# Taking the barriers out of a three-stage decoder-layer kernel: weights as bf16 images in DRAM, SBUF slots reused tile by tile

## The reference

```python
h = rmsnorm(x, norm1_w);  z = h @ w_in                    # (S, 5632)
q, k, v, xr, yr, ga, gr = split(z)                        # 512,512,512,1024,1024,1024,1024
o_attn = moba_attention(rmsnorm(q), rmsnorm(k), v, rel_bias)   # 8 heads of 64, block 256, own block + top 3 past blocks
xr = causal_depthwise_conv(xr);  o_rnn = rg_lru(xr) * gelu(yr) # linear recurrence over the tokens
merged = sigmoid(ga + b0) * (o_attn @ w_proj_attn) + sigmoid(gr + b1) * (o_rnn @ w_proj_rnn)
x = x + merged @ w_out
x = x + square(relu(rmsnorm(x, norm2_w) @ w_ff1)) @ w_ff2      # 1024 -> 4096 -> 1024
```

## Time and profile before

| | us |
|---|---|
| median of 3 runs (2818.44 to 2821.68) | 2819.83 |
| the profiled execution, its own time | 2818.97 |
| its span on the slowest core (core 4) | 2817.3 |
| spans of the 8 cores | 2802.9 to 2817.3 |
| PE busy | 2478.8 (88%) |
| ACT busy | 1573.3 (56%) |
| DVE busy | 1112.8 (39%) |
| POOL busy | 287.8 (10%) |

### The profile page before, as it was taken

The page is one execution under the profiler, slowest core; times in us unless marked ns, Lnnn a source line. Parts: engine busy times, 40 slices in busy tenths (PEclk is TensorE's granted clock), DMA queues, the critical chain, the costliest instruction groups (busy, mean ns, idle before and its releaser), DMA issues.

```text
span 2817.3 us, 37218 instructions; the slowest of 8 cores (2802.9 to 2817.3 us)
## 1 busy us (share of the span) xinstructions
PE 2478.8 (88%) x12206; PEld 1116.8 (40%) x12434; DVE 1112.8 (39%) x1860; ACT 1573.3 (56%) x2339; POOL 287.8 (10%) x310
## 2 busy tenths in 40 slices
PE   1888899999988458999999999956999999999999
PEld 0444444444433113444443443422444444444444
DVE  1764444342200166677677677321122122221221
ACT  0567788989899377788779778132122132231220
POOL 1000000000000122222112112020001011010110
PEclk9999999999999779999999999977999999999999
DMA  6211101100000690211220220297211211112101
GB/s 106 90 57 49 42 16 53 38 16 31 5 8 1 138 135 1 83 40 46 80 83 16 68 83 9 89 181 134 75 46 45 83 38 60 60 45 75 46 30 53
DMA packets 66921, 165.82 MB, mean 59 GB/s; under 512 B 7283, under 2 KB 27932, under 8 KB 65692
## 3 DMA queue, kind: packets, MB, share of 16 engines
q1 hardware_dynamic: 38028, 129.60, 14.3%
q0 software_dynamic: 28704, 33.82, 8.3%
HBM read 151.07 MB, written 46.15 MB: 70 GB/s over the span
## 4 chain that ended last, share of the span: by engine, by line
PE 76%; ACT 9%; issue 5%; DMA 4%; DVE 4%; another core or an unknown queue 1%; POOL 0%; SPq 0%; ACTq 0%; DVEq 0%; POOLq 0%
PE bank L422 76%; ACT arena L422 9%; DVE arena L422 4%; DMA arena<-w_in 1%; ACT L422 1%; DMA arena<-x 1%; DMA arena<-out 1%; DMA arena<-scr_w 1%; POOL arena L422 0%; DMA arena<-c_G 0%; SPq L427 0%; DMA scr_w<-arena 0%; ACTq L247 0%; DMA scr_o<-arena 0%
## 5 line engine op out<-in xcount | busy, mean ns | idle before, releaser
L422 PE MATMUL bank<-arena 128*128 128x512 bf16 (+8 forms) x12206 | 2478.8, 357 | 334.5 <-DVE arena L422 112.8
L422 PEld LDWEIGHTS bank<-arena 128*128 128x128 bf16 (+4 forms) x12434 | 1116.8, 99 | 1695.9 <-issue 622.5
L422 ACT ACTIVATE arena<-bank 128x1024 bf16<-128x1024 f32 (+3 forms) x1024 | 786.0, 795 | 725.7 <-PE bank L422 717.5
L422 ACT ACTIVATE arena<-arena 128x512 f32<-128x512 f32 (+5 forms) x642 | 375.9, 599 | 105.4 <-DMA arena<-x 52.6
L422 DVE TENSOR_TENSOR arena<-bank,arena 64x512 bf16<-64x512 f32 (+3 forms) x218 | 137.0, 641 | 664.0 <-PE bank L422 598.1
L422 DVE SCALAR_TENSOR_TENSOR arena<-arena 128x512 f32<-128x512 f32 (+2 forms) x321 | 276.2, 866 | 232.1 <-ACT arena L422 227.1
L422 DVE TENSOR_TENSOR arena<-arena 128x512 bf16<-128x512 f32 (+2 forms) x324 | 212.3, 656 | 326.6 <-ACT arena L422 316.2
L422 POOL TENSOR_TENSOR arena<-arena 128x512 bf16<-128x512 f32 x176 | 212.2, 1206 | 1222.2 <-ACT arena L422 458.2
L422 DVE SCALAR_TENSOR_TENSOR arena<-arena,bank 128x512 f32<-128x512 f32 x256 | 173.1, 681 | 125.8 <-ACT arena L422 65.8
L422 ACT ACT_TABLE_LOAD x129 | 165.5, 1283 | 96.8 <-POOL arena L422 48.0
L422 ACT ACTIVATE arena<-bank,arena 128x512 f32<-128x512 f32 x256 | 166.4, 684 | 61.6 <-PE bank L422 39.9
(11 more groups left out here) (17 smaller groups left out, 69.8 us busy)
## 6 DMA issues: line engine op xcount, KB each, us to landing
arena<-x SPq DMA_DIRECT2D x64, 512.0 KB, 4.2
out<-arena SPq DMA_DIRECT2D x64, 512.0 KB, 2.9
arena<-out SPq DMA_DIRECT2D x64, 512.0 KB, 4.2
arena<-w_ff POOLq DMA_DIRECT2D x16, 1024.0 KB, 75.7
arena<-w_in POOLq DMA_DIRECT2D x11, 1024.0 KB, 30.8
scr_h<-arena SPq DMA_DIRECT2D x32, 256.0 KB, 3.2
arena<-scr_h SPq DMA_DIRECT2D x8, 1024.0 KB, 4.9
scr_o<-arena SPq DMA_DIRECT2D x8, 512.0 KB, 3.8
```

Of the source, the lines that this page charges most:

```text
L422: return P.add(eng, lambda e, m=meth, kw=kw: getattr(e, m)(**kw), reads, writes, cost=cost, fam=fam)
```

## The change

What it does, part by part:

1. **Images.** 27 DRAM tensors `img_*` are added. For every weight except `wqkv` and the small block-diagonal ones, one DMA on the POOL queue reads the float32 weight and writes it as bf16 to its image, DRAM to DRAM. They are issued during stage A: the one for tile t waits until the keys of tile t-1 are made. `load_w` later moves an image into SBUF as it is, from the SP queue.
2. **No barriers.** Every SBUF region has a fixed offset and a second or third tenant. `P.alias` names, for each new tile, the old tiles whose readers and writers its first write must wait for.
3. **Loads placed ahead.** Four of the recurrence's weight tiles, `wbda`, `wbdi` and the first `hTs` are loaded in chunk 6 of stage A; the rest of stage B's weights right behind the last attention result. `W1` is loaded in chunks 6 and 7 of stage B, `W2` behind stage B's last stores. The front end of stage C's chunk 0 (`FECt`) stands between the gatings of chunk 7.
4. **Start.** The loads of x tiles 0 and 1 stand first on SP. The four loads and matmuls of the bias table become one load of 1 MB and four matmuls behind the first FE. `c_E` (the 16 rows that carry the block mask into the keys) and `pvec` move behind the first FE.
5. **Cost model.** The scheduler's costs of ACT and POOL instructions change (89 ns for a scale or bias that is a tile), and its model of DMA: one pipe for each queue, at 140 B/ns for POOL and 340 B/ns for the others, in place of one common pipe at 270. So the order of instructions differs in all stages.

```diff
+            for k in writes:
+                for old in self.alias.pop(k, ()):
+                    j = last_w.get(old)
+                    if j is not None:
+                        d.add(j)
+                    d.update(readers.get(old, ()))
...
-                    xfer = nb / 270.0
-                    t0 = max(st + cost, dma_pipe)
-                    dma_pipe = t0 + xfer
+                    xfer = nb / (140.0 if e == 'gpsimd' else 340.0)
+                    t0 = max(st + cost, dma_pipe[e])
+                    dma_pipe[e] = t0 + xfer
...
+        def load_w(nm):
+            img, dst = image[nm]
+            dma('sync', dst.rearrange("p a b -> p (a b)"), img, 'ld_' + nm, ['im_' + nm], [nm])
...
+                for nm, img, src in imaged[t:t + 1] if t else ():
+                    dma('gpsimd', img, src, 'im_' + nm, ['kT%d' % (t - 1)], ['im_' + nm])
...
+            FE(0, 0)
+            for g in range(4):
+                op('tensor', 'matmul', ['hk', 'Js'], ['B%d' % (3 + g)], out=bankf[3 + g], lhsT=Js, rhs=hk[:, 2 * g:2 * g + 2, :],
+                   start=True, stop=True)
...
+            dma('sync', kT[64:80, :, :], cE_d.rearrange("n (h s) -> n h s", h=NH, s=S), 'c4', [], ['kTE'])
+            dma('sync', pvec, pvec_d.rearrange("p (t j) -> p t j", t=8, j=11), 'c0c', [], ['pvec'])
+            for tl in range(1, TPC):
                 FE(0, tl)
...
+                    if c == NCH - 2 and h == 5:
+                        dma('sync', nw, nw_d[:, D:2 * D], 'c0g', [], ['nw', 'nw2'])
+                        for nm in ('wr0', 'wr2', 'wr1', 'wr3'):
+                            load_w(nm)
...
         if 2 in phases:
-            P.barrier()
-            AR.reset(mP)
...
+                    if c == NCH - 1:
+                        if m == 0:
+                            for tl in range(3):
+                                load_xC(0, tl)
+                        if m % 2 == 1:
+                            FECt(0, m // 2)
...
+                        if m < 4:
+                            load_w('w1_%d' % (m + 4))
...
         if 3 in phases:
-            P.barrier()
-            AR.reset(mP)
...
+            for g in (0, 1, 2, 6, 7, 3, 4, 5):
+                load_w('w2_%d' % g)
```

More of the change, by code:

```diff
@@ L399, in op @@
                     if eng == 'scalar':
-                        cost = nel * 0.8333 + 105.0
-                        if 'out' in kw and kw['out'].dtype == F32 and nel >= 256:
-                            cost += 70.0
+                        cost = nel * 0.8333 + (98.0 if ref_ap.dtype == BF16 else 170.0)
+                        for o_ in ('scale', 'bias'):
+                            if o_ in kw and not isinstance(kw[o_], float):
+                                cost += 89.0
                     elif eng == 'vector':
@@ new lines, in build_nc @@
+        oaTs = [AR.alloc([4, CH], BF16), AR.at(RA + 36 * K, [4, CH], BF16)]
+        assert AR.off <= RK + 32 * K
+        ornTs = [AR.at(RK + 32 * K, [8, CH], BF16), AR.at(RA + 8 * K, [8, CH], BF16)]
+        wpa = AR.at(RV, [4, D], BF16)
+        wpr = AR.at(RV + 8 * K, [8, D], BF16)
+        wo = AR.at(RV + 24 * K, [8, D], BF16)
+        mT = AR.at(RV + 40 * K, [8, CH], BF16)
+        xres = [AR.at(RA + (24 + 4 * i) * K, [D], F32) for i in range(3)]
+        kTh = ['kTh%d' % h for h in range(4)]
@@ new lines, in build_nc @@
+        for i in range(8):
+            P.alias['ornT0_%d' % i] = ['kTh4']
+            P.alias['ornT1_%d' % i] = list(A_keys)
+            P.alias['mT%d' % i] = list(V_keys)
+        for nm in ('wr7', 'BhT1', 'oaT1', 'Bxres0', 'Bxres1', 'Bxres2'):
+            P.alias[nm] = list(A_keys)
+        for nm in ('wpa', 'wpr', 'wo'):
+            P.alias[nm] = list(V_keys)
+        orn0 = ['ornT0_%d' % i for i in range(8)]
+        orn1 = ['ornT1_%d' % i for i in range(8)]
+        mTk = ['mT%d' % i for i in range(8)]
@@ L451, in build_nc @@
[L451 to L456, removed]
@@ L457, in build_nc @@
-        m0 = AR.mark()
+        AR.reset(m0)
         tabx = AR.alloc([NH], F32)
@@ new lines, in build_nc @@
+        for j in range(3):
+            dma('gpsimd', wqkv[j], w_in_v[:, :, j * 512:(j + 1) * 512], 'wqkv%d' % j, [], ['wqkv%d' % j])
+        for t in range(NT):
+            op('gpsimd', 'memset', [], ['V%d' % t], ap=Vg[:, t, 1:12:3, :], constant=1.0)
+        casts = []
+        for g in (0, 2, 1, 3, 4, 6, 5, 7):
+            casts.append(('wr%d' % g, w_in_v[:, :, 1536 + g * 512:1536 + (g + 1) * 512], wr[g]))
+        casts.append(('wpa', wpa_d.rearrange("(t p) c -> p t c", p=128), wpa))
+        casts.append(('wpr', wpr_d.rearrange("(t p) c -> p t c", p=128), wpr))
@@ new lines, in build_nc, with x1_tile, load_xC @@
+            dma('sync', oaTs[0].rearrange("p a b -> p (a b)"), scr_o[0], 'oa0', ['scr_o0'], ['oaT0'])
+            for nm in ('wr4', 'wr6', 'wpa', 'wpr', 'wr5', 'wr7', 'wo'):
+                load_w(nm)
+        def x1_tile(c, tl):
+            if c == 0:
+                return xsF[tl], ('Cx0', 'Cy0', 'Cy1', 'Cx0')[tl]
+            return xsC[tl % 2], 'Cx%d' % (tl % 2)
+        def load_xC(c, tl):
+            xt, xk = x1_tile(c, tl)
+            t = c * TPC + tl
+            dma('sync', xt, out_tiles[t], 'x' + xk, ['out%d' % t], [xk])
```

373 lines of the change are left out of this document (212 added, 161 removed).

## The result

The changed kernel takes 2769.6 us (2768.6 to 2773.0) beside 2820 us: a ratio of 0.982, with an interval of 0.980 to 0.985. It is faster by 50 us where 118 were forecast, and 18 us above the top of the range. The profiled execution took 2773.0 us, its span is 2771.5.

The account below looks back on a forecast made before the run. Long stretches were taken as near a limit of PE and ACT, gains lying in three dents. Terms -62 - 44 - 22 + 10 = -118 us took the 2817.3 us span to 2699.3, so 2702 as measured time; range 2660 to 2752.

Parts of the forecast that it names:

- End of B: Border of stages B and C: the gap and the late weights and lower clock behind it go, -62 us (-35 to -64).
- Border of A and B: Between attention and stage B: the 31.0 us weight wait and 13 us of further waits go, -44 us (-31 to -51).
- Start: Start of stage A: x lands earlier, other q and k begin at 56 instead of 73.5 us; -22 us (-8 to -49).
- The casts: Stage A: casts delay x loads by 2.5 us for four tiles, +10 us (0 if hidden, +40 if every load is late).
- Order: All stages: new costs move instructions but the limits stay, 0 us (-10 to +10).
- rival 3: Traffic costs more: casts at +40, image or `W2` loads hold x or gating 15 us more; 2747 us, chance 0.19.
- The recorded bounds: Whole kernel: the terms' bounds taken together were said to give 2647 and 2796 us.

Follow-up runs that it names:

- e10: Changed kernel with a barrier behind stage B's last store again, and the loads of x, `W1`, `W2` and stage C's first four front ends behind it: 2808.1 us.
- e9: Changed kernel with a barrier behind attention again, and the loads of stage B's weights, first h and block-diagonal weights behind it: 2828.0 us, a single run.
- e15: As e9, but the four small loads of the block-diagonal weights stay ahead of the border as in the changed kernel: 2811.3 us.
- e3: Changed kernel with the scheduler's ACT and POOL costs and its DMA transfer model put back to those of before, casts in place: 2709.5 us.
- e8: As e3, but without images or their casts, weights loaded straight from float32 as in e4: 2717.1 us.
- e4: Changed kernel without images or their casts: each weight loaded from its float32 source, converted on the way, on POOL's queue: 2760.5 us.
- e11: Changed kernel with only the list of casts turned, so that the eight of `w_ff2` come first: 2783.0 us.

## Why the prediction was wrong, by its steps

- *End of B, -62*: right. From B's last matmul to the end 72.9 us went; the front ends that moved made B's last chunk 11.5 us longer (first store to first store 72.1 us, before 60.6) where 4.0 was counted. Together -61. The size is partly luck: the gap, the clock and the waits gave 7 us more than counted behind the border, and the front ends cost 7.5 more ahead of it. `W2`'s eight loads, issued together, landed in a median of 13.2 us and the x behind them in 20 to 21, so that ACT didn't wait for it at all, where 2 us were counted. Undoing it cost 38 us (e10): 52 behind the border, less the front ends' share in B's last chunk.
- *Border of A and B, -44*: right, -47 (138 to 90.9). Undoing it cost 58 us in e9's one execution, 26 of them by small loads that the kernel before didn't have behind images, and 42 in e15.
- *Start, -22*: near in its landmarks, wrong in what they were worth. `pvec` landed at 53 us (47 was taken), the second q was squared at 61 (56). The bias table's load took 19.1 us (10) and was issued at 20.6 (24.6), `c_E` took 27.8 (16.1). Without casts chunk 0 was stored 12 us earlier than before in this order, and stage A ended only 4.5 us earlier. In the old order it was 30 and 25 us. The prediction saw that the squares of tiles 3 and 4 stood ahead of the other q and k, and still counted the start apart from the order.
- *The casts, +10*: here it failed. They cost 62 us. The 2.5 us for each of four tiles should have been five waits of 9 to 12 us and two of 2 to 3: the load of x took 14.7 us, where 9.5 had been read from a row with 16 casts in flight and the price was then taken as 5.3 of lateness less some lead. Under the casts no lead was left, so in five tiles nearly the whole rise (4.2 to 14.7) came out as waiting, 59 us in sum, and stage A, whose PE stands behind ACT, lost as much. The page's rule (the Trainium skill, "DMA: Bandwidth & Descriptors", section "Issuing engines are not separate DMA queues") pointed the right way, and the +40 by it was nearer than the 10 taken, though still short.
- *Order, 0*: failed as well. It was read from stretches that are near a limit, 200 us onwards; the loss arose ahead of them. A plan that thinks x there in 3.5 us puts each square as early as it can, and on an in-order engine all behind it waits. Price: 20 us without casts, 55 with them, by the transfer model for the most part (47 of the 60 us of e3 in time). No rival joined the two, though rival 3 had the casts' side of it at +40. Of its 15 us of waits for image loads 3.8 came, for `wpa` at 1005 us.

With the terms as measured (-61 - 47 - 5 + 62) the sum is -51. The difference of the spans is -46; the 5 us that are left over lie in the middle of B, and no term named them. The recorded bounds add to 2646 at the low end and not 2647, which changes nothing.

Open: why e8 was 34 us quicker than e4 behind stage A (both have the 18.95 us wait in B's last chunk); how the engine costs lose their 11 to 14 us; what part of the 62 us is PE's lower clock. A third buffer for x, which would give the loads another tile of lead, wasn't tried.

## What to carry to other kernels

Background traffic is free only while every load beside it keeps its lead: read the landing of the load that an in-order engine waits for, under full DMA share, multiply its rise by the tiles whose lead is shorter, and put the traffic where nothing loads (27 casts moved into attention's pauses, with the plan repaired: 71 us). A scheduler's transfer model must let queues delay each other; one that is near for a single queue (it plans a load of x at 3.5 us, alone it took 4.2) and blind to the others gave a worse order than a cruder shared pipe. And when a term is small "because it is hidden" and another is zero "because order doesn't matter", ask what they do together: here they were 62 and 20 us, and a plan that reckons with the casts leaves 27 of the first.

## What the runs showed of the hardware that was not expected

- A load of 512 KB that lands in a median of 4.2 to 4.9 us without casts beside it (before, e4, e8) took 13.6 to 14.7 us beside casts from DRAM to DRAM, whether these were of 1 KB or 2 KB rows (changed, e3, e11).
- Loads of 64 KB in short rows on another queue took 21 to 33 us to land beside 13 MB of images, and 3.5 us behind them (e9).
- A cast of 1 MB with none other close landed in 8 to 11 us (changed, behind 440 us), six close together beside loads of x in a median of 22.6.
